# A hybrid decoder block on one core: twelve of 384 dense tokens leave the expert products and take their pre-activations by fetched rows

## The reference

```python
q = (h @ w_query).reshape(T, 8, 2, 128)
s = einsum('thpd,hpkd->thpk', q, sub_keys)            # 2 x 128 scores per head
s1, i1 = top_k(s[:, :, 0], 16); s2, i2 = top_k(s[:, :, 1], 16)
best, pos = top_k(s1 + s2 of all 256 pairs, 16)        # 16 of 16384 experts per head
idx, gate = i1 * 128 + i2 at pos, softmax(best)
act = einsum('td,thkd->thk', h, expert_u[idx])
out = einsum('thk,thkd->td', gate * gelu(act), expert_v[idx])
```

## Time and profile before

| | |
|---|---|
| median of three runs | 4233.51 us (4231.85 to 4234.92) |
| profiled execution, its time | 4232.76 us |
| its span, first to last instruction | 4231.0 us |
| TensorE busy | 4203.4 us, 99% of the span |
| GpSimd busy | 2354.3 us, 56% |
| VectorE busy | 1960.7 us, 46% |
| ScalarE busy | 1420.4 us, 34% |
| bytes moved by DMA | 860.05 MB, 203 GB/s over the span |

### The profile page before, as it was taken

How to read it: one execution, slowest core, us unless ns; L and a number is a source line. 1 busy time by engine, 2 the same in 40 slices (tenths; PEclk the granted TensorE clock), 3 DMA queues, 4 the chain that set the end, 5 groups by cost and what they waited for, 6 DMA issues and landing times.

```text
span 4231.0 us, 52876 instructions
## 1 busy us (share of the span) xinstructions
PE 4203.4 (99%) x20315; PEld 3648.8 (86%) x20315; DVE 1960.7 (46%) x2518; ACT 1420.4 (34%) x1791; POOL 2354.3 (56%) x705
## 2 busy tenths in 40 slices
PE   8999999999999999999999999999999999999999
PEld 7888888877787888888999999999998888888887
DVE  5400045122122022038857666666735666666665
ACT  4322222233233122132345555555522222222223
POOL 4444433433333434433466666666667777777774
PEclk9999999999999999999999999999999999999999
DMA  4233322222223333322348888888878888888883
GB/s 179 92 124 121 123 95 90 91 89 80 89 90 134 121 112 111 108 90 86 124 161 301 310 320 310 320 311 321 316 293 316 323 321 312 333 314 320 321 324 132
DMA packets 204603, 860.05 MB, mean 203 GB/s; under 512 B 17072, under 2 KB 99312, under 8 KB 114928
## 3 DMA queue, kind: packets, MB, share of 16 engines
q1 hardware_dynamic: 64368, 459.30, 29.9%
q0 software_dynamic: 36864, 268.45, 15.9%
q10 hardware_dynamic: 103296, 131.44, 8.7%
HBM read 796.22 MB, written 62.91 MB: 203 GB/s over the span
## 4 chain that ended last, share of the span: by engine, by line
PE 97%; POOL 1%; DMA 1%; ACT 1%; DVE 1%; issue 0%; ACTq 0%; DVEq 0%; SPq 0%
PE bank L1756 17%; PE bank L1757 17%; PE bank L1758 17%; PE bank L1780 8%; PE twin L1780 8%; PE bank L2079 4%; PE bank L2081 4%; PE bank L2083 4%; PE twin L2081 4%; PE twin L2083 4%; PE twin L2079 4%; PE twin L2050 1%; PE twin L1757 1%; PE twin L1758 1%; PE twin L1756 1%; POOL low L490 1%
## 5 line engine op out<-in xcount | busy, mean ns | idle before, releaser
L490 POOL TENSOR_TENSOR low<-raw,high 128x2048 fp32r<-128x2048 f32 x431 | 1999.2, 4639 | 1753.3 <-ACT high L583 1752.6
L583 ACT ACTIVATE high<-raw 128x2048 fp32r<-128x2048 f32 x432 | 828.5, 1918 | 2372.4 <-PE bank L1758 1178.1
L1756 PE MATMUL bank<-x_high,high 128*128 128x384 f32 (+1 forms) x3680 | 1322.4, 359 | 1.9 <-POOL low L490 1.9
L1757 PE MATMUL bank<-x_low,high 128*128 128x384 f32 (+1 forms) x3680 | 1319.3, 359 | 0.0
L1758 PE MATMUL bank<-x_high,low 128*128 128x384 f32 (+1 forms) x3680 | 1319.3, 359 | 0.0
L1756 PEld LDWEIGHTS bank<-x_high,high 128*128 128x128 f32 x3680 | 691.0, 188 | 66.6 <-issue 2.2
L1758 PEld LDWEIGHTS bank<-x_high,low 128*128 128x128 f32 x3680 | 690.8, 188 | 63.6
L1757 PEld LDWEIGHTS bank<-x_low,high 128*128 128x128 f32 x3680 | 691.0, 188 | 62.9
L1626 DVE SCALAR_TENSOR_TENSOR fetched<-fetched,wide 128x2048 f32<-128x2048 f32 x128 | 289.9, 2276 | 44.4 <-DMA fetched<-expert_u,slot_i 44.4
L2079 PE MATMUL bank<-high,a_high 128*128 128x512 f32 x768 | 298.9, 389 | 0.6 <-POOL low L490 0.6
L2083 PE MATMUL bank<-high,a_low 128*128 128x512 f32 x768 | 298.8, 389 | 0.0
(11 more groups left out here) (257 smaller groups left out, 4800.7 us busy)
## 6 DMA issues: line engine op xcount, KB each, us to landing
raw<-weights SPq DMA_DIRECT2D x432, 1024.0 KB, 4.8
act_dram<-act_out ACTq DMA_DIRECT2D x128, 192.0 KB, 4.0
retrieved_dram<-stage ACTq DMA_DIRECT2D x48, 512.0 KB, 5.0
act_in<-act_dram ACTq DMA_DIRECT2D x32, 768.0 KB, 7.8
gates_in<-retrieved_dram ACTq DMA_DIRECT2D x32, 768.0 KB, 9.1
gates_dram<-sgu_act ACTq DMA_DIRECT2D x32, 256.0 KB, 2.0
gate_in<-gates_dram ACTq DMA_DIRECT2D x32, 256.0 KB, 2.6
xa<-x ACTq DMA_DIRECT2D x1, 4096.0 KB, 16.0
```

Of the source, the lines that this page charges most:

```text
L490: nc.gpsimd.tensor_tensor(low[:, slot, :], raw[:, slot, :], high[:, slot, :].bitcast(F32), ALU.subtract).then_inc(low_done, 1)
L583: nc.scalar.activation(high[:, slot, :], raw[:, slot, :], ACT.Copy).then_inc(high_done, 1)
L1756: nc.tensor.matmul(o, high[:, slot, w], x_high[:, 0:tiles, k, :], start=(k == 0), stop=False)
L1757: nc.tensor.matmul(o, high[:, slot, w], x_low[:, 0:tiles, k, :], start=False, stop=False)
```

## The change

The last two tokens of every 64 in the dense tiles (62, 63, 126, 127 of each tile; 12 tokens, `EXTRA`) leave the products against `expert_u`. `column(..., tiles=3)` names 6 runs of 62 columns, in its moving operand and in its PSUM output, which makes 372. The 12 tokens' pre-activations are taken as rows: 10 partitions hold 10 slots of one token at once, so 13 more fetches of 120 rows (`EXTRA_ROWS`) and 13 more dots serve 12 x 128 slots; the order of the now 141 fetches is `ROW_ORDER`.

To lay that out, ScalarE's queue issues, behind the first query head, one save of two tiles of `xa` and six small stores of h rows; in the lead a load of `wide_extra`; at the end of the lead six small stores of expert numbers and gates, and after the first `gate_parts` two loads. In the trail it takes Gelu of the 13 columns, stores the weights, loads `xa` back (2 MB) and loads `extra_w` turned, one 4-byte element at a time (128 x 12). Three more gate steps, behind trail units 5, 6 and 7, spread those weights over the keys into `extra_stage`; `product` copies them over the 12 columns of `act_in` and multiplies the rest in two instructions in place of one. Semaphores and allocations that only carry this are left out here.

```diff
+FEW, SPAN = 2, 64
+SPANS = P // SPAN
+EXTRA = DENSE_T * SPANS * FEW
+EXTRA_SLOTS = P // EXTRA
+EXTRA_ROWS = -(-SLOTS // EXTRA_SLOTS)
+U_ROWS = SLOTS + EXTRA_ROWS
+EXTRA_STEPS = EXTRA // WTOK
+EXTRA_UNIT = 5
...
-    return min(SLOTS, max(0, unit - FIRST_STEP) * SLOTS // (ETILES - FIRST_STEP - 4))
+    return min(U_ROWS, max(0, unit - FIRST_STEP) * U_ROWS // (ETILES - FIRST_STEP - 4))
+def row_order():
+    order, slots, extras = [], 0, 0
+    for n in range(U_ROWS):
+        if extras < EXTRA_ROWS and slots == 16 + 6 * extras:
+            order.append((True, extras))
+            extras += 1
+        else:
+            order.append((False, slots))
+            slots += 1
+    return order
+ROW_ORDER = row_order()
+LAST_EXTRA = ROW_ORDER.index((True, EXTRA_ROWS - 1)) + 1
...
+        wide_extra = at("wide_extra", [P, D], F32, region_a)
+        all_slots = at("all_slots", [P, DENSE_T, SLOTS], U32, region_a + 8 * 1024)
+        all_gates = at("all_gates", [P, DENSE_T, SLOTS], F32, region_a + 10 * 1024)
+        all_weights = at("all_weights", [P, EXTRA_ROWS], F32, region_a + 12 * 1024)
+        extra_stage = at("extra_stage", [P, P, EXTRA], F32, region_b + 24 * 1024)
...
-            def fetch_u(slot):
-                if slot >= ROW_BUFS:
-                    pool.wait_ge(rows_used, slot - ROW_BUFS + 1)
-                fetch_row(expert_u, slot, slot % ROW_BUFS)
+            def fetch_u(n):
+                extra, which = ROW_ORDER[n]
+                if n >= ROW_BUFS:
+                    pool.wait_ge(rows_used, n - ROW_BUFS + 1)
+                if extra:
+                    if which == 0:
+                        pool.wait_ge(extra_in, 2 * 16)
+                    parts = slice(0, EXTRA * EXTRA_SLOTS)
+                    nc.gpsimd.indirect_dma_start(
+                        fetched[n % ROW_BUFS][parts, :], None, expert_u,
+                        bass.IndirectOffsetOnAxis(extra_i[parts, which:which + 1], 0)).then_inc(rows_in[n % ROW_BUFS], 16)
+                else:
+                    fetch_row(expert_u, which, n % ROW_BUFS)
             def fetch_v(slot):
                 b = slot % VALUE_BUFS
                 if slot >= VALUE_BUFS:
-                    pool.wait_ge(rows_used, SLOTS + slot - VALUE_BUFS + 1)
+                    pool.wait_ge(rows_used, U_ROWS + slot - VALUE_BUFS + 1)
                 elif b < ROW_BUFS:
-                    pool.wait_ge(rows_used, SLOTS - ROW_BUFS + b + 1)
+                    pool.wait_ge(rows_used, U_ROWS - (U_ROWS - 1 - b) % ROW_BUFS)
...
             query_head(True)
+            act.dma_start(xa_dram.rearrange("t p d -> p t d"), xa[:, 0:2, :]).then_inc(xa_saved, 16)
+            for g in range(SPANS):
+                token = SPAN * (g + 1) - FEW
+                for t in range(DENSE_T):
+                    first = (t * SPANS + g) * FEW
+                    rows_of = xb[token:token + FEW, t, :].unsqueeze(1).to_broadcast([FEW, EXTRA_SLOTS, D])
+                    act.dma_start(extra_x_dram[first:first + FEW], rows_of).then_inc(extra_x_saved, 16)
...
-            def gate_parts(which, token):
+            def gate_parts(which, token, *gates):
                 act.wait_ge(hits_made, made.next())
                 for n in range(WTOK):
-                    for part, gate in enumerate((gate_high, gate_low)):
+                    for part, gate in enumerate(gates or (gate_high, gate_low)):
...
             act.dma_start(gffn_all[:], g_ffn_row.partition_broadcast(P)).then_inc(gffn_in, 16)
+            act.wait_ge(xa_saved, 16)
+            act.wait_ge(extra_x_saved, 16 * DENSE_T * SPANS)
+            act.dma_start(wide_extra[0:EXTRA * EXTRA_SLOTS, :],
+                          extra_x_dram.rearrange("i j d -> (i j) d")).then_inc(extra_x_in, 16)
             pairs(2, 2)
             act.wait_ge(peer_diff, 1)
             nc.scalar.activation(all_best[:], all_best[:], ACT.Exp).then_inc(peer_exp, 1)
             pairs((LEAD - 6) // 2, 6)
+            act.wait_ge(extra_named, 1)
+            for dram, tile in ((extra_i_dram, all_slots), (extra_gate_dram, all_gates)):
+                for g in range(SPANS):
+                    token = SPAN * (g + 1) - FEW
+                    act.dma_start(dram[:, 0:SLOTS].rearrange("(t g f) s -> g f t s", g=SPANS, f=FEW)[g],
+                                  tile[token:token + FEW, :, :]).then_inc(extra_saved, 16)
+                if EXTRA_SLOTS * EXTRA_ROWS > SLOTS:
+                    act.dma_start(dram[:, SLOTS:], tile[0:EXTRA, 0, 0:EXTRA_SLOTS * EXTRA_ROWS - SLOTS]).then_inc(
+                        extra_saved, 16)
...
             gate_parts(0, 0)
+            act.wait_ge(extra_saved, 16 * 2 * (SPANS + (1 if EXTRA_SLOTS * EXTRA_ROWS > SLOTS else 0)))
+            for dram, tile in ((extra_i_dram, extra_i), (extra_gate_dram, extra_gate)):
+                act.dma_start(tile[0:EXTRA * EXTRA_SLOTS, :],
+                              dram.rearrange("i (j g) -> (i j) g", j=EXTRA_SLOTS)).then_inc(extra_in, 16)
...
+                if n == 0:
+                    act.wait_ge(rows_used, LAST_EXTRA)
+                    nc.scalar.activation(extra_act[0:EXTRA * EXTRA_SLOTS, :], extra_act[0:EXTRA * EXTRA_SLOTS, :],
+                                         ACT.Gelu).then_inc(extra_acted, 1)
+                if n == 1:
+                    act.wait_ge(extra_weighted, 1)
+                    act.dma_start(extra_w_dram, all_weights[0:EXTRA * EXTRA_SLOTS, :]).then_inc(extra_w_saved, 16)
+                if n == 2:
+                    act.wait_ge(extra_w_saved, 16)
+                    act.dma_start(xa[:, 0:2, :], xa_dram.rearrange("t p d -> p t d")).then_inc(xa_back, 16)
+                    turned_w = extra_w_dram.rearrange("(i j) g -> i (j g)", j=EXTRA_SLOTS)[:, 0:SLOTS]
+                    act.dma_start(extra_w[:], turned_w.rearrange("i s -> s i"), allow_slow_non_contiguous=True).then_inc(extra_w_in, 16)
+                if n == 4:
+                    act.wait_ge(extra_w_in, 16)
+                    nc.scalar.activation(extra_high[:], extra_w[:], ACT.Copy).then_inc(extra_rounded, 1)
                 expert_unit(n % 2, ETILES - TRAIL + n)
+                if EXTRA_UNIT - 1 <= n < EXTRA_UNIT - 1 + EXTRA_STEPS:
+                    q = n - EXTRA_UNIT + 1
+                    gate_parts((STAGES * STEPS + q) % 2, q * WTOK, extra_high, extra_low)
...
+            dve.wait_ge(extra_x_in, 16)
+            dve.wait_ge(slots_done, 1)
+            nc.vector.tensor_copy(all_gates[:], all_best[:, 0:DENSE_T, :, :].rearrange("p t h k -> p t (h k)"))
+            nc.vector.scalar_tensor_tensor(out=all_slots[:], in0=expert_i[:, 0, 0:DENSE_T, :], scalar=float(KEYS),
+                                           in1=expert_i[:, 1, 0:DENSE_T, :], op0=ALU.mult,
+                                           op1=ALU.add).then_inc(extra_named, 1)
+            dve.wait_ge(gffn_in, 16)
+            parts = slice(0, EXTRA * EXTRA_SLOTS)
+            nc.vector.tensor_tensor(wide_extra[parts, :], wide_extra[parts, :], gffn_all[parts, :], ALU.mult)
             dve.wait_ge(slots_kept, 1)
-            dve.wait_ge(gffn_in, 16)
...
+            def extra_gate_sum(q):
+                dve.wait_ge(step_mm, STAGES * STEPS + q + 1)
+                if q == 0:
+                    dve.wait_ge(stage_out[1], 16 * PIECES * (STAGES // 2))
+                nc.vector.tensor_reduce(extra_stage[:, :, q * WTOK:(q + 1) * WTOK].rearrange("p i t -> p t i"), parts,
+                                        AX_X, ALU.add).then_inc(step_out, 1)
+            def extra_weights():
+                dve.wait_ge(extra_acted, 1)
+                rows_of = slice(0, EXTRA * EXTRA_SLOTS)
+                nc.vector.tensor_tensor(all_weights[rows_of, :], extra_act[rows_of, :], extra_gate[rows_of, :],
+                                        ALU.mult).then_inc(extra_weighted, 1)
+            def extra_rest():
+                dve.wait_ge(extra_rounded, 1)
+                then(nc.vector.tensor_tensor(extra_low[:], extra_w[:], extra_high[:].bitcast(F32), ALU.subtract))
...
+            def dot(n):
+                extra, which = ROW_ORDER[n]
                 where = take()
-                nc.vector.scalar_tensor_tensor(out=where[:], in0=where[:], scalar=1.0, in1=wide[:], op0=ALU.mult,
-                                               op1=ALU.mult,
-                                               accum_out=slot_act[:, slot:slot + 1]).then_inc(rows_used, 1)
+                if extra:
+                    rows_of = slice(0, EXTRA * EXTRA_SLOTS)
+                    nc.vector.scalar_tensor_tensor(out=where[rows_of, :], in0=where[rows_of, :], scalar=1.0,
+                                                   in1=wide_extra[rows_of, :], op0=ALU.mult, op1=ALU.mult,
+                                                   accum_out=extra_act[rows_of, which:which + 1]).then_inc(rows_used, 1)
...
+                if trail == 1:
+                    extra_weights()
+                if EXTRA_UNIT - 1 <= trail < EXTRA_UNIT - 1 + EXTRA_STEPS:
```

(47 more changed lines are left out.)

72 lines of the change are left out of this document (55 added, 17 removed).

## The result

The kernel became slower, by a little: 4240.23 us median of 16 runs (4233.97 to 4242.23) against 4232.04 of 16 runs of the kernel before (4227.42 to 4234.92), ratio 1.0017 with a 95% interval of 1.001 to 1.0024. Forecast were 4208 us. The profiled execution took 4241.92 us (span 4240.0) against 4232.76 (span 4231.0): 9.0 us more span. It lies near the slow end of the kernel's 16 runs; what that means for the trail is told under the experiments.

A forecast was written before the change was run, and what follows sets the result against it. TensorE was taken as the bound, 97% of the chain; 30.7 - 1.2 - 1.4 - 0.7 - 2.0 = 25.4 us off 4232.76 gave 4207.4, as a median 4208. Its own range was 4202 to 4217, with rivals 4202 to 4219.

The forecast's parts named there:

- What the products give: Expert products on TensorE: 12 columns less save 5.0 ns each, 0.24 us a unit, 30.7 us over 128 units.
- Rival 2: TensorE handles runs in blocks, so 62 cost what 64 do: nothing off, 4.1 us added, 4238; chance 0.05.
- the fit: TensorE's products: one column a period at 2.4 GHz, 0.417 ns a column, with 13.3 ns fixed.
- the values: Values stretch: `product` becomes three instructions, perhaps 0.3 us more in each of 32 groups; cost nothing, bound 1 us.
- The trail's transfers: ScalarE's queue in the trail: `xa` and `extra_w` arrive late by 0 to 8 us, taken as 2.
- Rival 4: The trail's wait, or raw loads landing late in the fuller DMA, cost 10 to 18 us: 4222; chance 0.06.
- The 13 fetches and dots: Expert units: more two-dot units and DMA load, paid from low's 1.66 us of slack; cost taken as nothing.
- the three gate steps: Trail units: three more gate steps on TensorE at 0.47 us each, 1.4 us in all.
- setting up: Behind the first query head and around the lead: extra DMA issues and list work, 0 to 3.3 us, taken as 0.7.
- The DMA share of 0.91: Gated stretch: DMA traffic rises from 313 GB/s at a share of 0.85 to 336 GB/s at 0.91.
- VectorE's load: Gated stretch: VectorE's busy time goes from 568 us of 844.8 to 596 of 822.
- The 1.2 us that the lead was to lose of the gain: Lead: low sets the start of some units, so 1.2 us of the products' gain is lost; bounds 0 and 3.

The follow-up runs named there:

- the forms: A kernel computing nothing of the block, timing 20 forms of the product, 96 each: six runs of 62 take 173.3 ns, one run of 372 takes 170.0.
- the products alone: The kernel before with only the change's products of 372 columns in six runs of 62, the twelve tokens' activations left out: 4232.67 us, ratio 1.0001.

## Why the prediction was wrong

**What the products give** is the step that failed: "This holds if a run of 62 columns with a gap behind it costs what a run of 128 costs." It doesn't. The evidence named for it, four runs of 128 against one of 512, was right and too coarse: at 128 a break costs nothing, and a run of 62 costs what 64 do. The 30.7 us were 0, shown by the forms, by the products alone, and by the period after. The side that had been suspected, the PSUM output, is free; the one that had been cleared, the moving operand, is the cause. Rival 2 had this at a chance of 0.05 with the note that the fit knew only multiples of 128. That note was the reason to give it far more: a length and a run that no row shows leave the fit unproved for just the case that the change makes. Its time, 4238, came within 2.2 us of the median, and that nearness is luck: it added 4.1 us of costs, where the profiled execution has 1.4 + 3.8 + 8.6 = 13.8, less 4.0 at the start and 0.9 in the values.

**The trail's transfers** were the right place with the wrong event and too small a size. 2.0 us were taken (bounds 0 to 8) for a wait before the copy of `extra_w`. That wait took 0.57 us, and `extra_w` landed 22.5 us after its issue with 22.7 in hand, so the bytes were priced well; an ordinary issue on the same queue was held up for 13.47, and the trail lost 8.6 us beyond its gate steps in the profiled execution, and 1.4 to 11.0 in those of the five kernels with the same trail and periods. In two of these the priced wait was there after all, 7.32 and 6.13 us. A wait that had no term, for the save before `xa` can be issued, made a high up to 3.7 us late where the save took 13.8 us or more to land. The prediction asked who waits for the bytes and not who issues behind them. Rival 4, 10 to 18 us for the trail's and the raw loads' waits, was a fair description: 8.6 + 3.8 = 12.4 us, but it was priced against a gain of 30.7.

**The 13 fetches and dots**, taken at nothing, cost 3.8 us in the gated stretch. That a two-dot unit is paid in the slack of the low "in more units but not more deeply" held for the dots by themselves: with fetches over 128 partitions they cost 0.1 us. What it missed is that a fetch to 120 partitions isn't the row fetch of the trace: 0.52 for 0.31 us a packet, a weight load that landed after 11.2 us where at worst 9.1 were reckoned with, and a high too late for the 1.66 us to spare. By which way the fetch delays the high stays open: the load landed at 2500.76 and high began 1.76 us later with no releaser in the profile, and with 384 columns the load landed 1.6 us ahead of need, at 2498.34, and high was 1.80 us late all the same. So the load isn't what it waited for there; the packet of the instruction queue named above is the nearest candidate.

**Right** were the three gate steps (1.4 us, measured 1.4), and that setting up and the values cost about nothing: the lead's sixteen units take 137.47 us for 137.39. The DMA share of 0.91 was met by luck: it was forecast for 336 GB/s and came at 326, with packets that took longer. VectorE's load rose by 45 us where 28 were forecast: 30 for the 13 dots, and most of the rest in `gate_hits`, whose first instruction has a mean of 1762 ns for 1569. The 1.2 us that the lead was to lose of the gain had no gain to be lost from; with runs of 124 three kernels gained 0.75 to 1.31 us there of 16 x 0.11 = 1.8, so a part is lost there as the step says. A slip in the trail's sum: 1.57 MB in 13.7 us are 115 GB/s and not 120, which makes 22.7 us of the 21.7 and would have moved the bounds by 1.

The range, 4202 to 4219, was set by costs of some microseconds around a gain held as certain; the gain itself, at 30.7 us the largest term, had no bound between nothing and its whole except as rivals. Removing one's own largest term is the range that was missing.

## What to carry to other kernels

A saving read from a fit holds for the lengths and patterns that the fit has seen; if the change makes a new one (a short run, a length that is no multiple of 16), a probe of 20 forms at 17 us each settles it before anything is built. Cut columns in long runs. Give a large transfer and one of many small elements their own places on an engine's DMA queue: the next issue on it can be held up (4 to 15 us here), and the engine's work with it, whoever needs the data. Let a gather fill all 128 partitions even if some rows are thrown away. And where executions differ as much as here, look at several traces before a wait is given its price.

## What the runs showed that was not expected

- A product's moving operand in runs of 62 costs what runs of 64 do (173.3 ns), in one run of 372 170.0; one run of 376 costs as much as 384 (173.3), and one of 380 less than that (171.1). Six gaps of 2 columns in the PSUM output are free (170.0 either way).
- An issue on ScalarE's DMA queue took 13.47 us behind 2 MB and 1536 elements, 4.47 to 14.56 (the longest of each) in the other traces with both, and 3.70 with the elements gone.
- 8 KB packets of a gather over 120 partitions take 0.44 to 0.56 us each in the mean of a gather, over 128 partitions 0.31 to 0.41.
- Ten copies of four rows, written to DRAM from four partitions, held up two weight loads, which landed after 28.2 and 27.0 us, at a DMA share of 0.26 from 1900 to 1910 us; written once they made ScalarE wait for no load.
